# The dt columns leave their own matmuls and ride behind the values' weights, in matmuls of 272 columns

## What is computed

```python
h = rmsnorm(x, mix_norm_gain[l])
proj = h @ w_in[l]                     # 1024 tokens x 3344 columns
xbc, z, dt_raw, gu, gv, q, k, v = jnp.split(proj, split_points, axis=-1)
y_ssd = ssd_mixer(xbc, z, dt_raw, ...)     # dt_raw has 16 columns
...
dt = softplus(dt_raw + dt_bias)        # in ssd_mixer: step sizes, 2 directions x 8 heads
```

## Time and profile before

| | |
|---|---|
| median of 3 runs | 2715.11 us (2713.05 to 2715.75) |
| profiled execution | 2719.25 us, its span 2717.5 us |
| granted TensorE clock, mean | 0.985 of full speed |
| PE busy | 2595.5 us, 96% of the span |
| DVE, ACT, POOL busy | 55%, 33%, 27% |
| chain that ended last | PE 85%, DVE 8%, ACT 3% |

### The profile page before, as it was taken

How to read it: one execution, slowest core, us unless ns; L and a number is a source line. 1 busy time by engine, 2 the same in 40 slices (tenths; PEclk the granted TensorE clock), 3 DMA queues, 4 the chain that set the end, 5 groups by cost and what they waited for, 6 DMA issues and landing times.

```text
span 2717.5 us, 33701 instructions
## 1 busy us (share of the span) xinstructions
PE 2595.5 (96%) x13478; PEld 2197.6 (81%) x13478; DVE 1489.5 (55%) x1743; ACT 896.6 (33%) x1536; POOL 728.4 (27%) x388
## 2 busy tenths in 40 slices
PE   5999997899999999999999999888999999999998
PEld 5988986787888888888788899777878888888887
DVE  5366557836444444444564755587364444444455
ACT  3245555613221122211233465565132121122121
POOL 2232110023333333333323311100333333333331
PEclk9999999899999999999999999999999999999999
DMA  5433343121111111111122344422111111111111
GB/s 192 135 106 124 125 141 139 55 93 47 47 47 47 47 47 47 47 48 54 59 102 74 113 132 140 167 98 86 39 55 47 47 47 47 47 47 47 47 54 71
DMA packets 76349, 214.11 MB, mean 79 GB/s; under 512 B 5896, under 2 KB 30472, under 8 KB 74888
## 3 DMA queue, kind: packets, MB, share of 16 engines
q1 hardware_dynamic: 55432, 180.69, 19.8%
q10 hardware_dynamic: 20776, 31.39, 3.5%
HBM read 178.47 MB, written 33.59 MB: 78 GB/s over the span
## 4 chain that ended last, share of the span: by engine, by line
PE 85%; DVE 8%; ACT 3%; issue 2%; DMA 1%; POOL 0%; SPq 0%; ACTq 0%; DVEq 0%; PEld 0%; POOLq 0%; PEldq 0%
PE PS L467 22%; PE PS L464 22%; PE PS L468 21%; PE PS L534 3%; PE PS L537 3%; PE PS L538 3%; PE PS L693 2%; PE PS L682 2%; DVE ACC L1292 1%; PE PS L850 1%; DVE HL L1313 1%; PE PS L672 1%; PE PS L671 1%; DVE CV L1462 1%; ACT LG L1123 1%
## 5 line engine op out<-in xcount | busy, mean ns | idle before, releaser
L464 PE MATMUL PS<-HH,WH 128*128 128x512 f32 x1920 | 757.0, 394 | 4.9 <-issue 4.9
L467 PE MATMUL PS<-HL,WH 128*128 128x512 f32 x1920 | 756.9, 394 | 0.0
L453 POOL CAST WH<-RAW 128x1024 fp32r<-128x1024 f32 x192 | 237.3, 1236 | 1930.0 <-PE PS L464 1446.2
L468 PE MATMUL PS<-HH,WL 128*128 128x512 f32 x1920 | 752.0, 392 | 0.0
L455 POOL TENSOR_TENSOR WL<-RAW,WH 128x1024 fp32r<-128x1024 f32 x192 | 496.2, 2584 | 15.4
L1722 DVE TENSOR_TENSOR X<-PS,X 128x512 f32<-128x512 f32 x384 | 259.3, 689 | 374.3 <-PE PS L468 373.8
L464 PEld LDWEIGHTS PS<-HH,WH 128*128 128x128 f32 x1920 | 362.8, 189 | 87.3 <-issue 5.4
L468 PEld LDWEIGHTS PS<-HH,WL 128*128 128x128 f32 x1920 | 362.4, 189 | 80.1
L467 PEld LDWEIGHTS PS<-HL,WH 128*128 128x128 f32 x1920 | 362.8, 189 | 75.9
L1251 ACT ACTIVATE FPAD<-PS 128x512 f32<-128x512 f32 x176 | 102.6, 596 | 883.7 <-PE PS L468 883.7
L1740 DVE SCALAR_TENSOR_TENSOR CVV<-FPAD,PARM,CVV 128x1024 f32<-128x1024 f32 x44 | 95.3, 2167 | 377.4 <-ACT CVV L1257 377.4
(11 more groups left out here) (205 smaller groups left out, 3163.1 us busy)
## 6 DMA issues: line engine op xcount, KB each, us to landing
RAW<-wst SPq DMA_DIRECT2D x192, 512.0 KB, 3.5
TOE<-toe_d SPq DMA_DIRECT2D x64, 512.0 KB, 3.8
XBS<-xbc_d SPq DMA_DIRECT2D x24, 512.0 KB, 4.9
xspill<-X ACTq DMA_DIRECT2D x2, 4096.0 KB, 12.5
xbc_d<-CV ACTq DMA_DIRECT2D x16, 512.0 KB, 3.6
tok_d<-ST ACTq DMA_DIRECT2D x16, 512.0 KB, 2.8
ZG<-tok_d SPq DMA_DIRECT2D x16, 512.0 KB, 3.3
X<-xspill SPq DMA_DIRECT2D x4, 2048.0 KB, 7.3
```

The lines of the kernel that those rows point to most:

```text
L453: nc.gpsimd.tensor_copy(hi, RAW[:, hf, :]).then_inc(hi_done, 1)
L464: ins = nc.tensor.matmul(out, wh, xh, start=first, stop=False)
L467: nc.tensor.matmul(out, wh, xl, start=False, stop=False)
L468: return nc.tensor.matmul(out, wl, xh, start=False, stop=last)
```

## The change

Slot 0 of WH and WL gets blocks of 272 columns: 256 of the unit, then 16 of dt. DVE writes the dt weights' high and low parts into these gaps once in a layer. The values' unit (2) is in slot 0, and its matmuls take 272 columns instead of 256, so that dt comes out by tokens as the columns 256 to 271 of each tile's PSUM bank. DVE adds the bias from there, once for each tile, ahead of its subtraction. `dt_columns`, `dt_turn`, the tiles WD and DTF and the copy on ACT are gone. POOL's writes into slot 0 become four blocks of 256 columns in place of a run of 1024. Some small tiles change their place in SBUF. The core of the diff:

```diff
+DTW = 16
+W_PITCH = (UC + DTW, UC)
+W_AT = (0, KT * (UC + DTW))
...
-                        hi = WH[:, s, hf * 1024:(hf + 1) * 1024]
+                        hi, lo = (t[:, W_AT[s] + hf * 4 * W_PITCH[s]:W_AT[s] + (hf + 1) * 4 * W_PITCH[s]]
+                                  .rearrange("p (k n) -> p k n", k=4)[:, :, 0:UC] for t in (WH, WL))
...
-            def tokens_part(s, t, k, b, release=False):
+            def tokens_part(s, t, k, b, release=False, w=UC):
...
-                def dt_columns():
-
-                    pe.wait_ge(row_sb, 1)
-                    pe.wait_ge(wdt_ready, l + 1)
-                    pe.wait_ge(a_free, 4 + a0 + A_XBC - 2)
-                    for th in range(2):
-                        for k in range(KT):
-                            nc.tensor.matmul(PS[0:32, 2 + th, :], WD[:, k, :], HH[:, k, half(th)],
-                                             start=(k == 0), stop=False, skip_group_check=True)
-                            last = nc.tensor.matmul(PS[0:16, 2 + th, :], WD[:, k, 0:16], HL[:, k, half(th)],
-                                                    start=False, stop=(k == KT - 1), skip_group_check=True)
-                    last.then_inc(dtf_full, 1)
...
+                        if u == 2 and t == 0:
+                            pe.wait_ge(wdt_ready, l + 1)
+                        tokens_tile(a0, u * NT + t, u, t, UC + DTW if u == 2 else UC)
...
-                between = {0: dt_columns, 1: lambda: heads_turn(3), 2: dt_turn, 6: decays, 8: decays_turn}
+                between = {1: lambda: heads_turn(3), 6: decays, 8: decays_turn}
...
-                act.wait_ge(dtf_full, l + 1)
-                A(DTF[:], PS[0:32, 2:4, :].rearrange("p a b -> p (a b)"), ACT.Copy).then_inc(dtf_ready, 1)
...
                     dve.wait_ge(vh_ready, l * NT + t + 1)
+                    ins = TT(U[:, t, :], PS[:, A_BANK[2 * NT + t], UC:UC + DTW], par_("dt_bias"), ALU.add)
+                    if t == NT - 1:
+                        ins.then_inc(u_ready, 1)
                     TT(VX[:, t, :, AD:2 * AD], PS[:, A_BANK[2 * NT + t], 0:AW].rearrange("p (h e) -> p h e", h=AH_),
...
-                dve.wait_ge(dt_full, l + 1)
-                raw = PS[:, 4, 0:NT * 32].rearrange("p (t e) -> p t e", t=NT)
-                dstep.then(TT(U[:], raw[:, :, 0:16], par_("dt_bias").unsqueeze(1).to_broadcast((P, NT, 16)), ALU.add))
-                TT(U[:], U[:], raw[:, :, 16:32], ALU.add).then_inc(u_ready, 1)
```

More of the change, by code:

```diff
@@ L143, in trunk @@
         RAW = place("RAW", [P, 2, 1024])
-        WH = place("WH", [P, SLOTS, 2048], dt=F32R)
-        WL = place("WL", [P, SLOTS, 2048], dt=F32R)
+        WH = place("WH", [P, W_AT[1] + 2048], dt=F32R)
+        WL = place("WL", [P, W_AT[1] + 2048], dt=F32R)
         PARM = place("PARM", [P, NPAR])
@@ L148, in trunk @@
         QSL = place("QSL", [P, AH_, P], top[0], F32R)
-        WD = place("WD", [P, KT, 32], dt=F32R)
         U = place("U", [P, NT, 16])
         LDT = place("LDT", [P, NT, 16])
+        DT = place("DT", [P, NT, 16])
+        ACS = place("ACS", [P, NT, 16])
         VS = place("VS", [P, P], top[0])
-        DT = place("DT", [P, NT, 16])
+        DEC = place("DEC", [P, NT, 16])
         GSQ = place("GSQ", [P, UC], top[0])
[L155 to L159, removed]
         SPL = place("SPL", [P, NT, 16])
@@ L167, in trunk @@
         VR = place("VR", [P, NT])
+        MN = place("MN", [P, AH_], top[0])
+        RSUM = place("RSUM", [P, 2, AH_], top[0] + 32)
         YSS = place("YSS", [P, NT, 2])
+        RC = place("RC", [P, AH_], top[0])
         YR = place("YR", [P, NT, 2])
@@ L332, in own, with weight_block, dt_weights @@
             return slice(AD * (h % 2), AD * (h % 2) + AD)
+        def weight_block(w, s, a, n):
+            at = W_AT[s] + a // UC * W_PITCH[s] + a % UC
+            return w[:, at:at + n]
+        def dt_weights(w):
+            return w[:, 0:W_AT[1]].rearrange("p (k n) -> p k n", k=KT)[:, :, UC:UC + DTW]
         def per_head(t, w=HD):
@@ L450, in _ @@
                             pool.wait_ge(w_used, r * SLOTS + s + 1)
-                        hi = WH[:, s, hf * 1024:(hf + 1) * 1024]
+                        hi, lo = (t[:, W_AT[s] + hf * 4 * W_PITCH[s]:W_AT[s] + (hf + 1) * 4 * W_PITCH[s]]
+                                  .rearrange("p (k n) -> p k n", k=4)[:, :, 0:UC] for t in (WH, WL))
+                        raw = RAW[:, hf, :].rearrange("p (k n) -> p k n", k=4)
                         settle(pool)
-                        nc.gpsimd.tensor_copy(hi, RAW[:, hf, :]).then_inc(hi_done, 1)
+                        nc.gpsimd.tensor_copy(hi, raw).then_inc(hi_done, 1)
                         pool.wait_ge(hi_done, n + 1)
-                        nc.gpsimd.tensor_tensor(WL[:, s, hf * 1024:(hf + 1) * 1024], RAW[:, hf, :],
-                                                hi.bitcast(F32), ALU.subtract).then_inc(w_ready, 1)
+                        nc.gpsimd.tensor_tensor(lo, raw, hi.bitcast(F32), ALU.subtract).then_inc(w_ready, 1)
         @block.tensor
@@ L527, in first_unit @@
                                 last.then_inc(a_full, 1 + ct)
-            def tokens_part(s, t, k, b, release=False):
-                tok, cols = slice(t * P, (t + 1) * P), slice(k * UC, (k + 1) * UC)
+            def tokens_part(s, t, k, b, release=False, w=UC):
+                tok = slice(t * P, (t + 1) * P)
+                wh, wl = weight_block(WH, s, k * UC, w), weight_block(WL, s, k * UC, w)
                 xh, xl = HH[:, k, tok], HL[:, k, tok]
-                o = PS[:, b, 0:UC]
-                ins = nc.tensor.matmul(o, xh, WH[:, s, cols], start=(k == 0), stop=False)
+                o = PS[:, b, 0:w]
+                ins = nc.tensor.matmul(o, xh, wh, start=(k == 0), stop=False)
                 if release:
                     ins.then_inc(w_used, 1)
-                nc.tensor.matmul(o, xh, WL[:, s, cols], start=False, stop=False)
-                return nc.tensor.matmul(o, xl, WH[:, s, cols], start=False, stop=(k == KT - 1))
+                nc.tensor.matmul(o, xh, wl, start=False, stop=False)
+                return nc.tensor.matmul(o, xl, wh, start=False, stop=(k == KT - 1))
             def bank_ready(a0, f):
@@ L543, in bank_ready, with tokens_tile @@
                     pe.wait_ge(a_free, 4 + a0 + n)
-            def tokens_tile(a0, f, u, t):
+            def tokens_tile(a0, f, u, t, w=UC):
                 bank_ready(a0, f)
                 for k in range(KT):
-                    last = tokens_part(u % SLOTS, t, k, A_BANK[f], t == k == 0)
+                    last = tokens_part(u % SLOTS, t, k, A_BANK[f], t == k == 0, w)
                 last.then_inc(a_full, 1)
```

19 lines of the change are left out of this document (5 added, 14 removed).

## The result

The changed kernel takes 2720.74 us, the kernel before 2715.39 us, each the median of 22 runs on the same chips; the ratio is 1.0017 [1.0011, 1.0024], so + 4.6 us with an interval of 3.0 to 6.5 (the medians differ by 5.35). The prediction said 2719 (2711 to 2725). The profiled execution took 2717.43 us with a span of 2715.6 us, less than that of before: that one had two early stretches at the low clock, 3.4 us from 42.8 and 6.8 us from 63.3, which this one lacks. Such early stretches come and go from trace to trace, whatever the kernel. So the two traces are compared stretch by stretch, not by their ends.

What follows compares the result with a forecast made beforehand. PE bounds the kernel, busy 2595.5 of 2717.5 us. Per layer + 1.3 columns, - 0.7 turn, - 0.7 transposes, + 2.0 clock, 0 POOL make + 1.9; two layers + 3.8 on 2715.1 give about 2719 us, range 2711 to 2725.

Steps and rivals of the forecast that it cites:

- The wait: Before the queries' last turn, behind the first xbc tile: PE stands still about 6.7 us in each layer.
- E + 5.5: E is the first dt matmul's start, 114.92; without dt matmuls the first xbc tile ends 5.5 us later and PE waits.
- E + 12.2: Forecast release of the queries' last turn, in place of E + 12.89; 0.7 us of the 7.38 removed are left.
- the meeting of the transfers: Next weights' DMA joins the keys' DMA on the queues; keys land up to 1.5 us later, 1.2 taken.
- The addition of 16 columns: DVE's small addition ahead of its last subtraction delays the keys' chain; 0.1 us taken.
- The columns: Values' tiles: 16 more columns cost 7.0 ns a matmul, 192 matmuls, + 1.3 us a layer.
- The rival of free columns: Values' matmuls: the weight load sets the pace, so 16 more columns cost nothing; 2716.4 us, chance 0.16.
- The clock: After PE's pause at the queries' turn the clock falls to 0.50; 1.5 to 2.6 us a layer lost, 2.0 taken.
- POOL: Slot 0 written as four blocks: 0 to 0.7 us a layer, counting before the last XBR loads; 0 taken.
- Behind this place all engines follow PE's xbc tiles, so nothing gives it back or adds to it: Rest of the program behind the queries' turn: no further gain or loss, so the sum of + 3.8 us stands.
- turn earlier: Queries' last turn on PE starts at about E + 12.2 in place of E + 12.89: - 0.7 us a layer.
- dt's transposes gone: Eight small transposes between the second and third xbc tiles drop out of PE's queue: - 0.7 us a layer.

Runs made afterwards that it cites:

- the two shifts of 64 bytes: Kernel before, with WH and WL 64 bytes higher in one run, HH, HL, X and all behind them 64 bytes lower in the other: 2709.84 us (0.9976) and 2710.15 us (0.9977).
- the later turn: Changed kernel with the queries' last turn one xbc tile later on PE, and ACT's first xbc copies ahead of the queries' high parts: 2708.07 us, ratio 0.9964.
- 192 bytes: Kernel before, with four small tiles placed ahead of the weights, so WH and WL lie 192 bytes higher: 2738.44 us beside 2716.08, one run.

## Why the prediction was right, and where it was not

**The wait: right, its length a little long.** PE stands before the queries' turn from E + 5.5 on, for DVE's QL and behind it the keys' DMA, in both layers. The turn came at E + 11.19, not E + 12.2, so 1.7 us were left, not 0.7. The term that was off is the meeting of the transfers: 1.2 us taken, 0.12 measured. The assumption "if each queue takes the two in turn" failed; the weights' transfer was late, the keys' was not. The run with the dt matmuls cut has the same start of the turn within 0.1 us. The addition of 16 columns cost 0.1 as taken.

**The columns: right.** 8.2 ns a matmul in place of 7.0, 1.6 us a layer in place of 1.3. The rival of free columns fell, and with it the estimate from the Trainium skill (TensorE: Matmul & The Clock Gate, section "Back-to-back issue gap"): 115.8 ns for 272 columns, where the trace has 126.0.

**The clock: right.** 1.3 and 2.5 us lost, 2.0 taken for each. In which layer the long stretch falls changes from kernel to kernel.

**POOL: right on POOL, wrong on what the blocks do.** POOL's operations keep their length (2.35 and 2.42 us for WL in the values' part) and the wait for XBR is 3.6 us at the longest, 3.4 before; it was 3.0 with the blocks alone and 3.7 with the dt matmuls cut and no blocks, so the blocks don't show in it. But they were weighed for the engine that writes them and not for the engine that reads them, PE: 4.5 us a layer.

**The failed sentence: "Behind this place all engines follow PE's xbc tiles, so nothing gives it back or adds to it".** Both happened: PE's pace in slot 0 added 4.5 us a layer, and the norm gave 3.7 back (3.2 net of the 0.5 us of slower matmuls between its marks).

In one sum, us a layer, predicted and then measured:

| step | predicted | measured |
|---|---|---|
| wider matmuls | + 1.3 | + 1.6 |
| turn earlier | - 0.7 | - 1.7 |
| dt's transposes gone | - 0.7 | - 0.7 |
| clock, mean of the layers | + 2.0 | + 1.9 |
| blocks, on PE, outside the norm's marks | 0 | + 4.0 |
| stretch at the norm, between its marks | 0 | - 3.2 |
| sum | + 1.9 | + 1.9 |

Twice 1.9 is + 3.8; the ratio gives + 4.6 [3.0, 6.5]. The sum came out as forecast because the errors cancel: the turn gave 1.0 us more than its term, and against that stand 0.3 more for the columns and 0.8 from two terms that were not in the sum. That is luck. The run with the blocks for the values alone has neither of these two; it gives + 4.1 [1.1, 6.8] by its ratio, and there the prediction's own terms, with the 6.83 us of low clock that its trace has in both layers (2.5 us lost in each), make + 3.4. One difference is left out of the table: in layer 1 the queries' unit, in slot 1, takes 22.6 us in the three kernels with blocks throughout and 23.4 in the others with HH and the weights in their old places. In layer 0 the short pace of 113.5 ns comes with blocks and without, so what brings it is open.

**What is shown and what is argued.** Shown: the wait, by the cut matmuls and by the later turn; the blocks' effect on PE, by the blocks alone; that the distance between the operands changes the pace, by the two shifts of 64 bytes and by AHI1. That the blocks act on PE through this distance is argued from it. Argued, too: that the norm's gain comes from which of DVE's addition and POOL's cast starts first, which a slower PE shifts. All eleven kernels fit in both layers. In the three at 226.7 ns the cast starts 0.15 to 0.19 us ahead of the addition, in the four at 228.9 ns 0.06 to 0.07; these seven have 93.6 to 95.0 us between the marks. In the three at 231.6 ns the cast starts 0.05 to 0.08 us behind the addition, in the one at 232.3 ns 0.11; these four (after, blocks alone, later turn, 192 bytes) have 90.7 to 91.6. But no run moved the addition or the cast by itself. Open is also by which rule the pace hangs on the addresses: in slot 0 with blocks the distance changes from block to block, and the pace by block (from 230.8 to 232.7 ns) does not follow from the values seen at fixed distances.

## What to carry to other kernels

Before work is taken from a busy engine, follow the longest chain on the other engines that runs beside it; what that chain still needs is not gained, and a pause in its place costs clock on top. If the order is written by hand, move another piece of work into the gap in the same edit: here that turned + 4.6 us into - 9.8. And a new layout is to be weighed for each engine that reads it: read the distance between starts of the same instruction on both sides. Here 2.2 ns a matmul, on the thousands that have 512 columns, were worth 6 us, more than the change itself.

## What the runs showed of the hardware

- A 512-column matmul with another weight load before each took from 226.7 to 234.3 ns at the full clock (226.7, 228.9, 231.6, 232.3, 233.4, 234.3), and edits that change nothing but places in SBUF moved it. The same places also gave 232.3 and 233.3 ns in one kernel. The Trainium skill (TensorE: Matmul & The Clock Gate, section "Step-by-step: what each phase is for") says that loading the next tile's weights takes no SBUF read bandwidth from the running matmul. These runs don't show which mechanism is at work, but they show that the two operands' places are not independent of each other.
- The copy SBUF to SBUF, already under way, was held up by 0.12 us when the load from memory joined it on the same 16 DMA engines; the load took 5.0 in place of 3.7 us.
- A DVE addition or subtraction of 512 columns takes 0.68 us alone and up to 2.9 us while POOL converts weights beside it. Which of the two is the long one went by the start: the addition 0.07 us behind the cast took 1.50 us beside 1.04, the addition 0.07 us ahead of it 0.69 beside 1.52. Ahead of something that PE waits for, these 0.14 us went with 3 us.
- A pause of the same length brought the clock down for 3.41 us in one layer and for 6.83 in the other, in the same kernel, and in another kernel the other way round. A sum should carry a mean for such a term, and a range.
